# One pass over eight experts in the loop body, with the experts' rows spread by two fp32r products and weighted by VectorE

## Chip, cores, metric

The kernel runs on one core of a Trainium2 chip. The time is device microseconds of one execution; the kernel before took 3247.16 us in the median of three runs (3246.65 to 3254.41). The core has TensorE (PE), VectorE (DVE), ScalarE (ACT), GpSimd (POOL) and SyncE (SP), which here issues the weight transfers.

## The reference

The program is four transformer layers over 256 tokens of width 1024. Only the last part of the last layer matters here, a mixture of eight experts with the best two per token:

```
logits = h2 @ w_router                       # 256 x 8
top_logits, top_idx = top_k(logits, 2); top_w = softmax(top_logits)
for the tokens xs of each expert e:
    hid = silu(xs @ w_gate[e]) * (xs @ w_up[e])      # 1024 -> 3584
    y   = hid @ w_down[e]                            # 3584 -> 1024
    out[token] += y * top_w[token, e]
h = layer_norm(alpha * h + out)
```

Everything is fp32 in and out.

## The kernel before

**Weights.** All weights stream through the core in tiles of four 128-row blocks by 512 columns (1 MiB). SyncE issues one transfer a tile into a ring of four raw buffers (RAW, L611), once VectorE has used the tile that lay there (low_ready). fp32 products are made of fp32r parts: ScalarE rounds the tile to its high part (high_part, L1194), VectorE subtracts to get the low part (low_part, L1594), each into a ring of three (SPLIT). The activations are split the same way. TensorE then makes three products per 128x128 block: high by high (L641), low by high (L642), high by low (L643), that is 12 products of 128x512 a tile (tile_products).

**Route.** The route stage computes the logits, for each token the two experts, their weights (ROUTE[.., 2, ..]) and the token's slot in its expert's list (ROUTE[.., 3, ..]), and NPASS: 1 if no expert has more than 128 tokens, else 2. A pass takes at most 128 tokens of each expert.

**Experts.** One expert is 42 tiles: seven blocks of 512 hidden columns, each with two tiles of gate, two of up and two of down. The down tiles of a block come behind the gate and up tiles of the next one. All engines run the same loop (Fori) over pairs of experts: passes * 4 iterations with two experts written out in the body, PAIR = 84 tiles. m counts experts and is a register value plus a constant; so are the values of most waits. The ring positions don't depend on the iteration. SyncE computes the expert's index at run time.

For each expert, VectorE makes the choice matrix (choose, L2409): CHOICE[token, slot] is 1 where the token is in that slot. A second pair of operations multiplies it by the token's weight (CHOICEW, L2413). Behind the hidden product of block 1 it does this for the next expert. At the four last tiles of an expert TensorE gathers the next expert's rows, X times CHOICE, in two groups of 16 recorded products (L1106), and turns CHOICEW (L1114) into CHOICET, which ScalarE copies (L1541). ScalarE and VectorE split the gathered rows into XG high and low.

At the end of an expert ScalarE copies the down result from banks 6 and 7 to YE (L1571) and raises down_read. In the next expert's tiles 3 to 6, one step ahead of each, TensorE makes spread s: one fp32 product 128x512, CHOICET times half of YE, into bank 5 (L1121; it is recorded as two matmuls). VectorE adds the bank to MERGED (L2425), the accumulator of the layer. The last expert's four spreads follow the loop, into banks 0 to 3. In the first expert the spreads work on zeros, which route wrote by memset into YE and CHOICET (L2353, L2354).

**Order.** Each engine runs its own instruction stream in order, and semaphores join them. On ScalarE the copy to YE stands ahead of the high part of the next tile, number 44 counted from the expert's first; on VectorE the low part runs two tiles ahead of TensorE.

Of the kernel before, what the change touches and what calls it, by code (L numbers as in the profile page):

```python
# [26 lines left out]
P = 128  # L27
# [7 lines left out]
RAW = 4  # L35
# [236 lines left out]
def build(nc, a, out, const_at):  # L272

    stages = schedule()
    with ExitStack() as ctx:
# [163 lines left out]
        hid_turned = sem("hidden_turned")  # L439
        down_read = sem("down_read")  # L440
# [119 lines left out]
        PAIR = 2 * (3 * J * 2)  # L560
        SPREAD_AT = 3
        GATHER_AT = PAIR // 2 - 4
        assert PAIR % RAW == 0 and PAIR % SPLIT == 0

# [25 lines left out]
        def _(sp):  # L590
# [12 lines left out]
            for st in stages:  # L603
                if st["kind"] == "experts":
                    def load(h, expert, done=0):

                        tile = st["tiles"][h % (PAIR // 2)]
# [20 lines left out]
        def _(pe):  # L628
# [465 lines left out]
            def experts(st):  # L1094
# [15 lines left out]
                def turn_choice(m, bank=5):  # L1110
                    if bank == 5:
                        pe.wait_ge(gathered_read, m * 2 + 2)
                    for t in range(T):
                        tr = nc.tensor.transpose(PS[:, bank, t * P:(t + 1) * P], CHOICEW[:, t, :], ident)  # L1114
                    tr.then_inc(choice_turned, 1)

                def spread(m, half, s, bank=5):
# [3 lines left out]
                    nc.tensor.matmul(PS[:, bank, :], CHOICET[:, half, s // 2, :], YE[:, s % 2, :], start=True,  # L1121
# [7 lines left out]
                with pe.Fori(0, passes * (N_EXPERTS // 2)) as i:  # L1129
                    for half in range(2):  # L1130
                        m = i * 2 + half
                        for n, tile in enumerate(st["tiles"]):
                            h = STATIC + half * (PAIR // 2) + n
                            j = tile["block"]
                            par = (half * J + j) % 2
# [5 lines left out]
                            if SPREAD_AT <= n < SPREAD_AT + 4:  # L1141
                                spread(m, 1 - half, n - SPREAD_AT)
# [7 lines left out]
                            if turned_block:  # L1150
                                tb = turned_block["block"]
                                pe.wait_ge(xh_ready, m * J + tb + 3)
                                for x in range(4):
                                    tr = nc.tensor.transpose(PS[:, 4, x * P:(x + 1) * P],
                                                             HID2[:, (half * J + tb) % 2, x * P:(x + 1) * P], ident)
                                tr.then_inc(xh_turned, 1)
                            if tile["role"] != "down":
                                if tile["k"] == 0:
# [5 lines left out]
                                              tile["k"] == 0, tile["last"], i * PAIR)  # L1164
                            else:
                                if tile["first"]:
                                    pe.wait_ge(xh_copied, m * J + j + 1)
                                tile_products(h, tile, [PS[:, 6 + tile["half"], :]],
                                              lambda part, k, t: HIDT2[part][:, par, k, :], j == 0, j == J - 1, i * PAIR)
# [15 lines left out]
        def _(act):  # L1185
# [345 lines left out]
            def experts(st):  # L1531
                act.drain().then_inc(down_read, 1)

# [15 lines left out]
                with act.Fori(0, passes * (N_EXPERTS // 2)) as i:  # L1549
                    for half in range(2):  # L1550
                        m = i * 2 + half
                        for n, tile in enumerate(st["tiles"]):
                            h, j = half * (PAIR // 2) + n, tile["block"]
                            par = (half * J + j) % 2
                            if n in (GATHER_AT, GATHER_AT + 1):
                                gather(m + 1, n - GATHER_AT)
                            if n == GATHER_AT + 2:
                                copy_choice(m + 1, 1 - half)
                            turned_block = block_to_turn(st["tiles"], n)
                            if turned_block:  # L1560
                                tb = turned_block["block"]
                                act.wait_ge(xh_turned, m * J + tb + 1)
                                nc.scalar.activation(HIDT2[0][:, (half * J + tb) % 2].rearrange("p k s -> p (k s)"),
                                                     PS[:, 4, :], ACT.Copy).then_inc(xh_high, 1)
                            ahead = h + SPLIT - 1
                            high_part(STATIC + ahead, st["tiles"][ahead % (PAIR // 2)], (i * (PAIR // RAW), i * PAIR))
                            if tile["role"] == "gate" and tile["last"]:
                                act.wait_ge(tile_used, i * PAIR + STATIC + h + 1)
                                nc.scalar.activation(SG2[:, par], PS[:, par], ACT.Silu).then_inc(xsilu_ready, 1)
                        act.wait_ge(tile_used, i * PAIR + STATIC + (half + 1) * (PAIR // 2))  # L1570
                        nc.scalar.activation(YE.rearrange("p b c -> p (b c)"), PS[:, 6:8].rearrange("p b c -> p (b c)"),  # L1571
# [933 lines left out]
```

## Time and profile before

| | |
|---|---|
| median of three runs | 3247.16 us (3246.65 to 3254.41) |
| the profiled execution | 3250.54 us, its span 3248.7 us, mean granted clock 0.985 |
| TensorE busy | 3092.7 us, 95% |
| weight loads busy | 2526.1 us, 78% |
| VectorE busy | 2298.4 us, 71% |
| ScalarE busy | 1757.2 us, 54% |
| DMA | 697.25 MB, mean 215 GB/s |
| chain that ended last | PE 75%, DVE 10%, DMA 5%, ACT 4%, DVEq 3%, issue 3% |
| moe weight transfers | 114 gate, 112 up, 112 down, 1024 KB each |

The page's shares are means over the whole program. The experts stage begins near 2184 us and ends near 3232 us, so that it is a third of the span, and rows of that stage have to be asked for by their time. Matmul durations overlap: a 128x512 product is recorded with 390 ns, but one starts every 227 ns.

### The profile page before, as it was taken

To read this page: it belongs to the slowest core of one execution; us is meant where nothing else is said; L and a number is where in the kernel's file an instruction comes from. 1 tells how busy PE (TensorE), PEld (TensorE's weight loads), DVE (VectorE), ACT (ScalarE), POOL (GpSimd) and SP (SyncE) were. 2 spreads that over 40 slices of the span, in tenths; PEclk is the share of its full clock that TensorE was granted. 3 is DMA by queue.
4 is the path that set the end of the run, shared out by engine and by line. 5 is a ranking of instruction groups with operands and counts; after the bars stand their busy time and mean duration, and the time that the engine had idled before them with its cause. 6 is when DMAs were issued, how large, how long until landed. Compare 5 with 4: busy or idle time off the path is not lost.

```text
span 3248.7 us, 38581 instructions
## 1 busy us (share of the span) xinstructions
PE 3092.7 (95%) x15010; PEld 2526.1 (78%) x15010; DVE 2298.4 (71%) x2134; ACT 1757.2 (54%) x1647; POOL 46.1 (1%) x28
## 2 busy tenths in 40 slices
PE   8999999999998999999989999979999999999998
PEld 6777887877887787777878877767787787877876
DVE  7886556886556556765455667658887887887888
ACT  4564445465444444553334445536676676766765
POOL 0000000100000000000000000000000000000000
PEclk9999999999999999999999999989999999999999
DMA  6434555434555454335554543339998998999997
GB/s 242 143 130 145 187 183 175 159 117 135 183 185 188 157 169 156 130 112 180 189 168 157 181 154 123 113 118 339 334 362 304 350 354 302 358 338 312 364 327 266
DMA packets 351081, 697.25 MB, mean 215 GB/s; under 512 B 12225, under 2 KB 17217, under 8 KB 350785
## 3 DMA queue, kind: packets, MB, share of 16 engines
q1 hardware_dynamic: 347024, 687.75, 61.8%
q10 hardware_dynamic: 3888, 7.07, 0.7%
q8 instruction: 128, 2.10, 0.3%
q14 instruction: 41, 0.33, 0.0%
HBM read 693.73 MB, written 1.05 MB: 214 GB/s over the span
## 4 chain that ended last, share of the span: by engine, by line
PE 75%; DVE 10%; DMA 5%; ACT 4%; DVEq 3%; issue 3%; PEld 0%; ACTq 0%; POOL 0%; PEldq 0%; SPq 0%
PE banks L641 22%; PE banks L643 21%; PE banks L642 21%; DVE weights_low L1594 4%; ACT weights_high L1194 2%; DMA weights_raw<-in_moe_w_down_dram 2%; PE banks L796 1%; DMA weights_raw<-in_moe_w_up_dram 1%; DMA weights_raw<-in_moe_w_gate_dram 1%; PE banks L678 1%; PE banks L1106 1%; PE banks L1121 1%; PE banks L753 1%; ACT weights_transposed L1373 1%; PE banks L782 1%
## 5 line engine op out<-in xcount | busy, mean ns | idle before, releaser
L1594 DVE TENSOR_TENSOR weights_low<-weights_raw,weights_high 128x2048 fp32r<-128x2048 f32 (+1 forms) x658 | 1490.7, 2269 | 532.5 <-ACT weights_high L1194 526.8
L1194 ACT ACTIVATE weights_high<-weights_raw 128x2048 fp32r<-128x2048 f32 (+1 forms) x658 | 1247.7, 1898 | 578.4 <-PE banks L643 454.2
L641 PE MATMUL banks<-weights_high,h_transposed_high 128*128 128x512 f32 x2784 | 1122.6, 403 | 28.7 <-DVE weights_low L1594 15.3
L643 PE MATMUL banks<-weights_high,h_transposed_low 128*128 128x512 f32 x2784 | 1087.9, 391 | 11.5 <-issue 11.5
L642 PE MATMUL banks<-weights_low,h_transposed_high 128*128 128x512 f32 x2784 | 1086.0, 390 | 0.0
L641 PEld LDWEIGHTS banks<-weights_high,h_transposed_high 128*128 128x128 f32 x2784 | 527.5, 189 | 163.4 <-issue 23.5
L643 PEld LDWEIGHTS banks<-weights_high,h_transposed_low 128*128 128x128 f32 x2784 | 526.9, 189 | 123.8 <-issue 12.8
L642 PEld LDWEIGHTS banks<-weights_low,h_transposed_high 128*128 128x128 f32 x2784 | 527.9, 190 | 109.4 <-issue 8.6
L641 PE MATMUL banks<-weights_high,y_transposed_high 128*128 128x512 f32 x1096 | 433.5, 396 | 9.1 <-DVE y_transposed_low L2446 4.6
L643 PE MATMUL banks<-weights_high,y_transposed_low 128*128 128x512 f32 x1096 | 427.2, 390 | 0.0
L642 PE MATMUL banks<-weights_low,y_transposed_high 128*128 128x512 f32 x1096 | 427.0, 390 | 0.0
L641 PEld LDWEIGHTS banks<-weights_high,y_transposed_high 128*128 128x128 f32 x1096 | 205.8, 188 | 60.9 <-DVE weights_low L1594 7.3
L643 PEld LDWEIGHTS banks<-weights_high,y_transposed_low 128*128 128x128 f32 x1096 | 205.7, 188 | 43.7
L642 PEld LDWEIGHTS banks<-weights_low,y_transposed_high 128*128 128x128 f32 x1096 | 206.0, 188 | 40.6
L1368 ACT ACTIVATE scratch<-scratch,minus_row_max 128x256 f32<-128x256 f32 (+1 forms) x128 | 56.7, 444 | 67.4 <-DVEq L2033 67.4
L2478 POOL TENSOR_TENSOR rsqrt<-mean_squares,minus_half 128x2 f32<-128x2 f32 (+3 forms) x23 | 45.8, 1991 | 3195.7 <-DVE mean_squares L2259 1617.6
L1334 ACT ACTIVATE qk_transposed<-banks 128x512 f32<-128x512 f32 x68 | 38.8, 570 | 64.3 <-PE banks L737 60.0
L1307 ACT ACTIVATE projected<-banks 128x512 f32<-128x512 f32 x34 | 20.3, 596 | 97.3 <-PE banks L643 97.3
L1250 ACT ACTIVATE h_transposed_high<-banks 128x512 fp32r<-128x512 f32 x32 | 17.9, 596 | 95.6 <-PE banks L678 95.6
L1498 ACT ACTIVATE y_transposed_high<-banks 128x1024 fp32r<-128x1024 f32 (+1 forms) x22 | 22.2, 1007 | 87.4 <-PE banks L1044 87.4
L2319 DVE TENSOR_TENSOR y_transposed_low<-banks,y_transposed_high 128x1024 fp32r<-128x1024 f32 (+1 forms) x22 | 26.4, 1200 | 58.9 <-ACT y_transposed_high L1498 58.9
L796 PE MATMUL banks<-projected,weights_transposed 128*128 128x64 f32 (+1 forms) x384 | 49.7, 279 | 15.6 <-ACT weights_transposed L1373 15.6
(308 smaller groups left out, 2068.2 us busy)
## 6 DMA issues: line engine op xcount, KB each, us to landing
weights_raw<-in_w_in_dram SPq DMA_DIRECT2D x152, 1024.0 KB, 5.0
weights_raw<-in_moe_w_gate_dram SPq DMA_DIRECT2D x114, 1024.0 KB, 6.6
weights_raw<-in_moe_w_up_dram SPq DMA_DIRECT2D x112, 1024.0 KB, 6.5
weights_raw<-in_moe_w_down_dram SPq DMA_DIRECT2D x112, 1024.0 KB, 6.4
weights_raw<-in_w_up_dram SPq DMA_DIRECT2D x32, 1024.0 KB, 5.6
weights_raw<-in_w_down_dram SPq DMA_DIRECT2D x32, 1024.0 KB, 5.0
weights_raw<-in_ffn_w_gate_dram SPq DMA_DIRECT2D x10, 1024.0 KB, 5.1
weights_raw<-in_ffn_w_up_dram SPq DMA_DIRECT2D x10, 1024.0 KB, 5.1
```

The costliest lines, as they stand in the source:

```text
L641: nc.tensor.matmul(out_of[t], lhs(0, k, t), high[:, k], start=begin, stop=False)
L642: nc.tensor.matmul(out_of[t], lhs(0, k, t), low[:, k], start=False, stop=False)
L643: mm = nc.tensor.matmul(out_of[t], lhs(1, k, t), high[:, k], start=False, stop=end)
L678: tr = nc.tensor.transpose(PS[:, t["banks"][b], at:at + P], buf[t["src"]][:, i, t["cols"][k]:t["cols"][k] + P], ident)
L753: mm = nc.tensor.matmul(PS[:, 5 + h, cols], z[rows, q * P:(q + 1) * P], zk[rows, S:S + keys], start=True, stop=True)
L782: tr = nc.tensor.transpose(PS[:, 5 + h, i * P:(i + 1) * P], SM[:, h, i * P:(i + 1) * P], ident)
L796: mm = nc.tensor.matmul(PS[:, 7, o:o + vw], PT[:, h, (kt + t) * P:(kt + t + 1) * P], PR[:, kt, v0[h]:v0[h] + vw], start=kt == 0, stop=kt == t)
L1194: nc.scalar.activation(tile_view(WH, h % SPLIT, tile), tile_view(raw, h % RAW, tile), ACT.Copy).then_inc(high_ready, 1)
L1334: nc.scalar.activation(QKT[:, (n - 1) % 2, 0:cols], PS[:, bank, 0:cols], ACT.Copy).then_inc(qk_copied, 1)
L1368: nc.scalar.activation(probs, probs, ACT.Exp, bias=NMX[:, i:i + 1], accum_out=SUM[:, i:i + 1])
L1594: v.tensor_tensor(tile_view(WL, h % SPLIT, tile), tile_view(raw, h % RAW, tile), tile_view(WH, h % SPLIT, tile).bitcast(F32), ALU.subtract ...
L2478: nc.gpsimd.tensor_tensor(RSTD[:, 0:n], STAT[:, 0:n], MHALF[:, 0:n], ALU.pow).then_inc(rsqrt_ready, 1)
```

## The change

The loop body becomes all eight experts (PASS = 336 tiles, EXPERT = 42), and the loop runs once per pass, which here is once. The expert's index is then a constant for each transfer. The spread uses CHOICE without the weight, turned, in fp32r, and YE in a high part (ScalarE) and a low part (VectorE): two fp32r products in place of one fp32 product. VectorE multiplies by the weight while it accumulates. YE now lies in the upper halves of the HT buffers and CHOICET in a part of YT. The memsets in route go; zeroing by a multiplication with 0 stands at the head of the experts stage instead. down_read is raised by VectorE, behind its subtraction, which waits for the new semaphore down_high.

```diff
-        YE = PRf[:, 4096:5120].rearrange("p (b c) -> p b c", b=2)
+        YE = [h.rearrange("p k s -> p (k s)")[:, 1024:2048].rearrange("p (b c) -> p b c", b=2) for h in HT]
-        CHOICEW = PRf[:, 5376:5632].rearrange("p (t s) -> p t s", t=T)
-        CHOICET = PRf[:, 5632:6144].rearrange("p (b t s) -> p b t s", b=2, t=T)
+        CHOICET = YT[0].rearrange("p k s -> p (k s)")[:, 1024:1536].rearrange("p (b t s) -> p b t s", b=2, t=T)
...
-        PAIR = 2 * (3 * J * 2)
+        EXPERT = 3 * J * 2
+        PASS = N_EXPERTS * EXPERT
...
-                    with sp.Fori(0, passes * (N_EXPERTS // 2)) as i:
-                        for h in range(SPLIT - 1, PAIR + SPLIT - 1):
-                            load(h, (i * 2 + h // (PAIR // 2)) % N_EXPERTS, i * PAIR)
+                    with sp.Fori(0, passes) as i:
+                        for h in range(SPLIT - 1, PASS + SPLIT - 1):
+                            load(h, h // EXPERT % N_EXPERTS, i * PASS)
...
-                        tr = nc.tensor.transpose(PS[:, bank, t * P:(t + 1) * P], CHOICEW[:, t, :], ident)
+                        tr = nc.tensor.transpose(PS[:, bank, t * P:(t + 1) * P], CHOICE[:, t, :], ident)
...
-                    nc.tensor.matmul(PS[:, bank, :], CHOICET[:, half, s // 2, :], YE[:, s % 2, :], start=True,
+                    nc.tensor.matmul(PS[:, bank, :], CHOICET[:, half, s // 2, :], YE[0][:, s % 2, :], start=True, stop=False)
+                    nc.tensor.matmul(PS[:, bank, :], CHOICET[:, half, s // 2, :], YE[1][:, s % 2, :], start=False,
                                      stop=True).then_inc(spread_full, 1)
...
-                with pe.Fori(0, passes * (N_EXPERTS // 2)) as i:
-                    for half in range(2):
-                        m = i * 2 + half
+                with pe.Fori(0, passes) as i:
+                    for e in range(N_EXPERTS):
+                        m = i * N_EXPERTS + e
...
-                        nc.scalar.activation(YE.rearrange("p b c -> p (b c)"), PS[:, 6:8].rearrange("p b c -> p (b c)"),
-                                             ACT.Copy).then_inc(down_read, 1)
+                        nc.scalar.activation(YE[0].rearrange("p b c -> p (b c)"), PS[:, 6:8].rearrange("p b c -> p (b c)"),
+                                             ACT.Copy).then_inc(down_high, 1)
...
-                v.memset(YE, 0.0)
-                v.memset(CHOICET[:, 1], 0.0)
...
+                for part in YE:
+                    v.tensor_scalar(part.rearrange("p b c -> p (b c)"), MERGED[:, 0], 0.0, None, ALU.mult)
+                v.tensor_scalar(CHOICET[:, 1].rearrange("p t s -> p (t s)"), MERGED[:, 0, 0:T * P], 0.0, None, ALU.mult)
+                dve.drain().then_inc(down_read, 1)
...
-                    dve.drain()
-                    for t in range(T):
-                        v.tensor_scalar(CHOICEW[:, t], CHOICE[:, t], ROUTE[:, t, 2, bass.ds(at, 1)], None, ALU.mult)
                     dve.drain().then_inc(choice_ready, 1)
...
-                    v.tensor_tensor(acc, acc, PS[:, bank], ALU.add).then_inc(spread_read, 1)
+                    last = (m + T * N_EXPERTS - 1) % (T * N_EXPERTS)
+                    v.scalar_tensor_tensor(out=acc, in0=PS[:, bank], scalar=ROUTE[:, s // 2, 2, bass.ds(last, 1)], in1=acc,
+                                           op0=ALU.mult, op1=ALU.add).then_inc(spread_read, 1)
...
+                        dve.wait_ge(down_high, m + 1)
+                        v.tensor_tensor(YE[1].rearrange("p b c -> p (b c)"), PS[:, 6:8].rearrange("p b c -> p (b c)"),
+                                        YE[0].rearrange("p b c -> p (b c)").bitcast(F32), ALU.subtract).then_inc(down_read, 1)
```

## Rows read from the trace of the kernel before

**Rows 1.** page, 40 slices of the span: busy tenths of DMA
```profile
DMA  6434555434555454335554543339998998999997
```

**Rows 2.** windows from spread to spread: busy us by engine, clock, DMA share
```profile
2193.80:2323.30 129.50, 126.74 (x575) 102.17 (x574) 108.83 (x67) 89.80 (x61) 0.00 (x0) 1.00 0.96 341
2323.30:2457.60 134.30, 128.44 (x575) 103.34 (x574) 108.56 (x67) 92.22 (x62) 0.00 (x0) 0.99 0.94 334
...
2847.50:2983.90 136.40, 130.00 (x576) 102.82 (x575) 108.63 (x66) 92.24 (x62) 0.00 (x0) 0.99 0.94 328
2983.90:3111.00 127.10, 125.79 (x575) 102.40 (x574) 108.61 (x67) 89.73 (x61) 0.00 (x0) 1.00 0.97 342
```

**Rows 3.** waits, experts stage: total us, times, longest
```profile
DVE weights_low L1594 <- ACT weights_high L1194: 169.0, 242, 4.8
...
PEld banks L641 <- DVE weights_low L1594: 29.0, 42, 1.9
```

**Rows 4.** chain of waits, 2240 to 2266 us: start, us, what
```profile
2252.62 7.64 DMA weights_raw<-in_moe_w_down_dram
...
2260.28 1.93 ACT weights_high L1194
...
2262.23 2.30 DVE weights_low L1594
```

**Rows 5.** chain of waits at the three returns of the loop
```profile
2445.03 3.85 issue
...
2450.57 0.43 PE banks L641
...
2706.18 1.09 issue
...
2708.68 3.58 issue
...
2971.17 4.06 issue
```

**Rows 6.** windows of 20 us around a return, and without one
```profile
2439.00:2459.00 20.00, 15.75 (x60) 11.86 (x59) 11.18 (x6) 13.86 (x10) 0.00 (x0) 0.91 0.69 237
...
2309.00:2329.00 20.00, 20.00 (x87) 15.63 (x86) 17.24 (x10) 15.17 (x11) 0.00 (x0) 1.00 0.92 328
```

**Rows 7.** timeline at the choice, VectorE then TensorE
```profile
2214.16 0.60 DVE L2409 TENSOR_SCALAR projected<-constants,projected 128x128 f32<-128x128 f32 x2
2214.94 0.49 DVE L2413 TENSOR_SCALAR projected<-projected 128x128 f32<-128x128 f32 x2 [0.19 <-issue]
2215.62 4.49 DVE L1594 TENSOR_TENSOR weights_low<-weights_raw,weights_high 128x2048 fp32r<-128x2048 f32 x2 [0.19 <-issue]
...
2217.97 0.50 PE L641 MATMUL banks<-weights_high,h_transposed_high 128*128 128x512 f32 x1 [0.88 <-DVE weights_low L1594]
```

**Rows 8.** chain of waits at a spread
```profile
2323.47 0.86 PE banks L1121 x2
...
2324.80 0.23 PE banks L643
```

**Rows 9.** groups by line of VectorE: count, busy us, mean ns
```profile
L2319 DVE TENSOR_TENSOR y_transposed_low<-banks,y_transposed_high 128x1024 fp32r<-128x1024 f32 x21 | 25.7, 1225 | 57.5 <-ACT y_transposed_high L1498 57.5
...
L2425 DVE TENSOR_TENSOR merged<-merged,banks 128x512 f32<-128x512 f32 x36 | 24.6, 684 | 3.2 <-PE banks L1121 3.2
...
L2268 DVE SCALAR_TENSOR_TENSOR x_residual<-x_residual,rsqrt,scratch 128x512 f32<-128x512 f32 x16 | 11.3, 749 | 0.7
```

**Rows 10.** chain of waits in the route stage
```profile
2169.12 0.91 DVE projected L2353
```

**Rows 11.** timeline of VectorE after the loop
```profile
3234.72 0.69 DVE L2425 TENSOR_TENSOR merged<-merged,banks 128x512 f32<-128x512 f32 x1 [0.17 <-PE banks L1121]
```

**Rows 12.** DMA queues: packets, MB, share; 2190 to 2405 us, then 2405 to 3218
```profile
q14 instruction: 6, 0.05, 0.1%
...
q8 instruction: 37, 0.61, 0.3%
```

More of the change, by code:

```diff
@@ L559, in build @@
         STATIC = h
-        PAIR = 2 * (3 * J * 2)
+        EXPERT = 3 * J * 2
+        PASS = N_EXPERTS * EXPERT
         SPREAD_AT = 3
-        GATHER_AT = PAIR // 2 - 4
-        assert PAIR % RAW == 0 and PAIR % SPLIT == 0
+        GATHER_AT = EXPERT - 4
+        assert PASS % RAW == 0 and PASS % SPLIT == 0
         def tile_view(buffer, slot, tile):
@@ L605, in load @@
                     def load(h, expert, done=0):
-                        tile = st["tiles"][h % (PAIR // 2)]
+                        tile = st["tiles"][h % EXPERT]
                         src = a[tile["name"]][tile["layer"], bass.ds(expert, 1), tile["row"]:tile["row"] + tile["rows"] * P,
@@ L1141, in experts @@
                             if SPREAD_AT <= n < SPREAD_AT + 4:
-                                spread(m, 1 - half, n - SPREAD_AT)
+                                spread(m, 1 - e % 2, n - SPREAD_AT)
                             if n == GATHER_AT:
@@ L1163, in experts @@
                                 tile_products(h, tile, [PS[:, bank, :]], lambda part, k, t: XG[part][:, tile["k"] + k, :],
-                                              tile["k"] == 0, tile["last"], i * PAIR)
+                                              tile["k"] == 0, tile["last"], i * PASS)
                             else:
@@ L1548, in experts @@
                 passes = act.value_load(NPASS[0:1, 0:1], min_val=1, max_val=T)
-                with act.Fori(0, passes * (N_EXPERTS // 2)) as i:
-                    for half in range(2):
-                        m = i * 2 + half
+                with act.Fori(0, passes) as i:
+                    for e in range(N_EXPERTS):
+                        m = i * N_EXPERTS + e
                         for n, tile in enumerate(st["tiles"]):
-                            h, j = half * (PAIR // 2) + n, tile["block"]
-                            par = (half * J + j) % 2
+                            h, j = e * EXPERT + n, tile["block"]
+                            par = (e * J + j) % 2
                             if n in (GATHER_AT, GATHER_AT + 1):
@@ L1557, in experts @@
                             if n == GATHER_AT + 2:
-                                copy_choice(m + 1, 1 - half)
+                                copy_choice(m + 1, 1 - e % 2)
                             turned_block = block_to_turn(st["tiles"], n)
@@ L2430, in experts @@
                 passes = dve.value_load(NPASS[0:1, 0:1], min_val=1, max_val=T)
-                with dve.Fori(0, passes * (N_EXPERTS // 2)) as i:
-                    for half in range(2):
-                        m = i * 2 + half
+                with dve.Fori(0, passes) as i:
+                    for e in range(N_EXPERTS):
+                        m = i * N_EXPERTS + e
                         for n, tile in enumerate(st["tiles"]):
-                            h, j = half * (PAIR // 2) + n, tile["block"]
-                            par = (half * J + j) % 2
+                            h, j = e * EXPERT + n, tile["block"]
+                            par = (e * J + j) % 2
                             if SPREAD_AT <= n < SPREAD_AT + 4:
```

24 lines of the change are left out of this document (12 added, 12 removed).

## The prediction

> **What bounds the kernel now.** I read the page's row of DMA shares first, then the stage in eight equal steps, then who waits for whom, then the chain of waits inside one step, and last the edges of the loop. The reader is to see this. Up to about 2184 us the sixteen DMA engines are half busy; in the last third, the experts stage, they are at eight or nine tenths nearly all the time [rows 1]. That stage is the only thing that the change touches. From the first spread of one expert to that of the next there are seven stretches, of which the first two and the last two stand in [rows 2]. Four of the seven (129.5, 129.7, 126.5, 127.1 us, mean 128.2) hold no return of the loop. Three (134.3, 133.7, 136.4, mean 134.8) do. TensorE is busy nearly throughout, and DMA at 0.94 to 0.97.
>
> So two things bound one expert in turn. TensorE needs 504 products of 0.227 us (a 128x512 product takes 0.23 of the chain [rows 8]), which is 114.4 us, plus gather 3.6 (two groups of 1.78 us), turning the hidden block 7 x 0.36 = 2.5, turning the choice 0.14 and the spread 3.4: together some 124 us. DMA needs 42 tiles of 1 MiB. At 0.965 busy over 128.2 us [rows 2] that is 123.7 us of full work. The two floors are almost equal, and an expert takes 128.2 because each is late for the other in turn. In the DMA's part the ring of four raw tiles is what one sees: a transfer of 7.6 to 7.9 us, then ScalarE's rounding 1.93, VectorE's remainder 2.30, and the next transfer starts [rows 4]. That is 12.3 us for four tiles, 3.08 each, where TensorE would take 2.72. Around the gathers and spreads TensorE is the slower one and the DMA share falls to about 0.9 [rows 6]. VectorE waits for ScalarE's high parts for 169 us in all, and TensorE waits for VectorE's low parts for 29 us, 3.6 an expert [rows 3].
>
> **The loop's returns.** The body of the loop covers two experts, runs four times, and so returns three times. At each, TensorE stands with the reason "issue": nothing that another engine did ended it. It is 3.85, 3.58 and 4.06 us [rows 5], with a shorter piece before it (0.39, 1.09, 0.5). Behind it the clock is granted at half for 3.4 us (products at 0.43 instead of 0.23 us in the chain [rows 5]), which loses 1.7 us more. Sum: 4.24 + 4.67 + 4.56 + 3 x 1.7 = 18.6 us. The stretches say the same from outside: 3 x (134.8 - 128.2) = 19.8. The body becomes eight experts and NPASS is 1 here (336 tiles were run), so no return is left. But while TensorE stood, the DMA idled only in part: share 0.69, 0.66, 0.71 in 20 us around the returns against 0.92, 0.86, 0.92 at the same place of an expert without one [rows 6], 0.213 x 20 = 4.3 us each, 12.8 in all. The rest of the pause was used to fill the ring. The gain therefore lies between 12.8 and 19.8. I take 17, nearer the upper end, because TensorE is what works directly behind the return, with spreads to do.
>
> Two ScalarE table loads of 1.28 us per body go from eight to two; they lie beside TensorE's pause and I cost them at nothing of their own. They would matter only if ScalarE were late, and it waits for TensorE or DMA.
>
> **The spread.** One fp32 product 128x512 is recorded as two, 0.86 us in the chain [rows 8]. It becomes two fp32r products. The trace has no spread of that kind; its nearest rows are the weight products, which are fp32r of the same shape: 0.227 each, 0.453 for both. Bounds: 0.45 if it is like those, 0.86 if nothing is gained. I take 0.453, saving 0.41 x 4 = 1.65 us an expert, 13.1 us in the eight that run inside the loop.
>
> **VectorE.** Accumulating becomes a scalar_tensor_tensor with a column of weights. Its neighbours are tensor_tensor at 0.68 and, with a column, 0.75 us [rows 9]: 0 to 0.07 more, 36 times, 2.4 us at most, beside TensorE's next tile. The register work for the column runs in the queue ahead of the engine. New is the low part of the down result: 128x1024 from PSUM, 1.22 us [rows 9], once an expert. It waits for ScalarE's copy. Behind it on VectorE stands the low part of tile 44, and for that TensorE waits. If TensorE ends tile 41 at T, ScalarE's copy ends at T+1.03, the subtraction at T+2.3 (VectorE may still be in tile 43's low part until about T+1.7, then T+2.9), while the high part of tile 44, behind the same copy on ScalarE, ends at T+2.95. So the subtraction fills time in which VectorE waits anyway, and TensorE has tiles 42 and 43 in hand, 5.4 us. Cost 0. If that cover is gone it is 2.25 us an expert, 18 in all.
>
> Off VectorE goes the weighted choice: two 128x128 operations and a drain. The chosen pair starts at 2214.16, the weighted pair at 2214.94, the next low part at 2215.62 [rows 7], so 0.68 us go. This is on the path: TensorE stands for about 1.04 us behind that low part (0.88 shown by the row, since its last product's modelled end overlaps [rows 7]), and does so once in every expert. I expect 0.36 of it to stay: 8 x 0.68 = 5.4 us gained. Bounds 0 and 8.3.
>
> **Edges.** In the route stage a memset of 0.91 us [rows 10] and a smaller one behind it leave VectorE's path, about 1.1 us. Two zeroings of 128x1024 and one of 128x256 come before the first choice, where the first gather waits for them: 1.7 by estimate: the trace has no scaling of that size into such an operand; the subtraction of 128x1024 at 1.22 us [rows 9] is the upper bound of each large one, its half the lower, and I take near the lower with a drain. The first choice is 0.7 shorter. Sum 0, between -0.5 and +1.3. At the end, the last spread now waits for the subtraction too (+1.2), and VectorE's four accumulations, 0.86 apart today since it waits for each product [rows 11], come 0.65 apart: -0.8. Sum +0.5.
>
> **The sum.** TensorE's side: 17 + 13.1 + 5.4 - 0.5 = 35. What of the 18.5 us of spread and choice remains after the DMA? An expert without a return would need 128.2 - 2.3 = 125.9 us, and DMA cannot do it in less than 123.7. So it fits, but the part of an expert in which the ring fills gets 2.3 us shorter, and the DMA idles only 4.5 us an expert today. In that part the DMA is at 0.9, so of a microsecond saved there most is not yet a DMA microsecond; later, in the ring's own part, some is waited for again. I take 60 per cent, between 0 and 100: 11 us. Total 17 + 11 - 0.5 = 27.5, rounded 28. The profiled execution took 3250.5 us (span 3248.7), so 3222.5. It lies 3.4 us above the median of the runs shown (3247.2); the forecast for that median is **3219**. Its own range is 3211 to 3228.
>
> **Rivals.**
> (a) *The DMA takes back all but its own idling.* For it: share 0.965 already, the 12.3 us ring. Against: it does fall to 0.9 at the spreads. Gain 12.8, time 3234. Chance 0.20.
> (b) *All of TensorE's side counts.* For it: the ring is full after every slow part. Against: 29 us of waits for low parts are left over today. 19.8 + 18.5 - 0.5 = 37.8, time 3209. Chance 0.20.
> (c) *VectorE's new wait isn't covered.* Low part of tile 44 comes 2.25 us late each time and the weight column costs 0.07 x 36: 28 - 18 - 2.4 leaves 8, time 3239. For it: VectorE is at 0.84 of a stretch. Against: ScalarE's order above. Chance 0.06.
> (d) *The longer program makes the engines wait for their code; slower than before.* The queue that brings 8 KB packets of code (q14) moved 0.05 MB, six packets, in the first 215 us of the loop, and has no row at all from 2405 to 3218, whereas TensorE's (q8) goes on with 37 of 16 KB [rows 12]. ScalarE, VectorE and SyncE thus ran bodies two to four from code they held. Now they need 3 x 6 = 18 more packets. If each came as late as TensorE's page at a return (3.85 us [rows 5]) that is 69 us; with half of it covered by the two tiles in hand, 35, and 3219 + 35 = 3254. It decides from 28 / 18 = 1.6 us a packet. Against: the first two experts did fetch theirs, in 129.5 us for the first, the same as the 129.7 of the third, which did not. Chance 0.04.
>
> Rows 12 and the pauses of rows 5 belong together: code is brought in pages, and TensorE's alone is too long to be kept. [...]
>
> **Chances.** Forecast 0.50, (a) 0.20, (b) 0.20, (c) 0.06, (d) 0.04. Changes within 0.3 per cent, about 9.7 us, can't be told from none by a measurement of this kernel: 3237.4 is the border. Faster: 0.50 + 0.20 + most of (a), 0.17 = 0.87. Same: rest of (a) 0.03, (c) 0.05 = 0.08. Slower: (d) and what is left = 0.05. The range reaches from below (b) to just past (a): 3205 to 3237.
>
> **What would show it.** In the changed profile: no "issue" of 3 to 4 us on TensorE and no half clock between 2190 and 3220; spread products of the weight products' duration, two a spread, and a tile with a spread in it 0.41 us shorter; a stall of about 0.4 instead of 1.04 after the choice; a new 128x1024 subtraction eight times with nothing of TensorE or of the low parts waiting for it; DMA share at 0.97 or more in each stretch; experts of 125 to 127.5 us. Experts of 128 with more waits for DMA show (a). "Issue" on VectorE, ScalarE or the DMA queue's engine at regular places, with packets on q14, shows (d). The prediction is wrong if experts take under 124 us, which would mean that the DMA can do more than I take for full, or over 129.

## The result and the profile after

The changed kernel takes 3211.26 us (median of four runs, 3206.66 to 3215.40) against 3247.25 us beside it. The ratio is 0.9877 with a 95 per cent interval of 0.9857 to 0.9897, so it is faster by 1.2 per cent. The medians lie 36 us apart, the ratio makes it 40 us (33 to 46), and 28 were forecast. The two profiled executions have spans of 3248.7 and 3209.3 us, 39.4 us apart. The terms below are compared on these two.

The page of the changed kernel: span, busy time, the DMA's busy tenths in 40 slices (now nine from the twenty-ninth on, where [rows 1] had eights), and the queue that brings code to the engines other than TensorE.

```profile
span 3209.3 us, 37966 instructions
...
PE 3073.3 (96%) x15010; PEld 2523.9 (79%) x15010; DVE 2302.4 (72%) x2125; ACT 1750.2 (55%) x1641; POOL 46.1 (1%) x28
...
DMA  6434555443565554335555543338999999999997
...
q14 instruction: 55, 0.45, 0.0%
```

The seven stretches of the experts stage, cut from ScalarE's copy of one down result to that of the next (columns: length, PE, PEld, DVE and ACT busy, POOL, granted clock, DMA share, GB/s):

```profile
2312.40:2437.30 124.90, 124.65 (x575) 102.12 (x575) 109.38 (x66) 89.61 (x61) 0.00 (x0) 1.00 0.99 353
2437.30:2562.60 125.30, 124.63 (x576) 102.30 (x575) 109.20 (x66) 89.60 (x61) 0.00 (x0) 1.00 0.99 352
2562.60:2687.70 125.10, 124.72 (x576) 102.10 (x575) 109.17 (x66) 89.89 (x61) 0.00 (x0) 1.00 0.99 353
2687.70:2813.60 125.90, 124.98 (x575) 101.98 (x574) 109.22 (x66) 89.98 (x61) 0.00 (x0) 1.00 0.99 350
2813.60:2940.30 126.70, 124.76 (x575) 102.07 (x574) 109.34 (x66) 89.65 (x60) 0.00 (x0) 1.00 0.99 348
2940.30:3065.50 125.20, 124.67 (x576) 102.25 (x575) 109.23 (x66) 89.49 (x61) 0.00 (x0) 1.00 0.99 353
3065.50:3191.00 125.50, 124.69 (x574) 101.82 (x572) 109.13 (x66) 89.61 (x60) 0.00 (x0) 1.00 0.95 338
```

Three of the same cuts in the kernel before: one without a return of the loop, one with, and the last.

```profile
2315.20:2443.20 128.00, 126.39 (x575) 101.96 (x573) 108.60 (x67) 89.45 (x60) 0.00 (x0) 1.00 0.97 345
2443.20:2579.20 136.00, 128.92 (x576) 103.50 (x576) 108.80 (x67) 92.30 (x62) 0.00 (x0) 0.99 0.93 325
3103.00:3231.60 128.60, 126.63 (x574) 101.67 (x572) 108.83 (x67) 89.46 (x60) 0.00 (x0) 1.00 0.92 329
```

Before, the seven were 128.0, 136.0, 127.0, 133.3, 129.9, 133.6 and 128.6 us, 916.4 in all. Now they are 124.9 to 126.7, 878.6 in all. So 37.8 of the 39.4 us are here. The stretches are the better measure than the spans: what lies ahead of the experts stage, where the kernels differ only in how they clear YE and CHOICET, moves its start by up to 5.6 us from one profile to another (first gather at 2175.8 to 2181.4 us). Each kernel has one profile, and single stretches without a return differ by up to 3.5 us inside one profile (123.5 to 127.0 in one_product below), so that a sum of seven is good to a few us only. The clock column reads 1.00 in every stretch. The DMA share is 0.99, against 0.93 to 0.97 before, and in the last stretch, where the loads end, 0.95 against 0.92. This answers to [rows 2, 6].

Who waits for whom in the stage (total us, times, longest), against [rows 3]. The pauses of 3.6 to 4.1 us by "issue" of [rows 5] are gone; what is left of that kind sums to 2.9 us and is never longer than 0.5.

```profile
DVE weights_low L1594 <- ACT weights_high L1196: 127.2, 220, 3.1
...
PEld banks L642 <- DVE weights_low L1594: 20.8, 41, 1.6
...
PEld banks L642 <- issue: 2.9, 7, 0.5
```

The chain of waits at a spread. Two products of 0.23 us stand where [rows 8] had 0.86:

```profile
2323.60 0.23 PE banks L644
2323.82 0.23 PE banks L1122
2324.05 0.23 PE banks L1123
2324.28 0.23 PE banks L642
```

VectorE's timeline at the choice, and TensorE's behind it, against [rows 7]. From the choice to the next low part it is 0.80 us instead of 1.46, and TensorE's stall has shrunk to 0.21 us by the row (0.37 from start to start, where it was 1.04):

```profile
2338.55 0.68 DVE L2454 TENSOR_TENSOR projected<-projected,banks 128x512 f32<-128x512 f32 x1
2339.14 0.60 DVE L2411 TENSOR_SCALAR projected<-constants,projected 128x128 f32<-128x128 f32 x2
2339.94 4.50 DVE L1594 TENSOR_TENSOR weights_low<-weights_raw,weights_high 128x2048 fp32r<-128x2048 f32 x2 [0.20 <-issue]
```

```profile
2342.29 0.50 PE L642 MATMUL banks<-weights_high,h_transposed_high 128*128 128x512 f32 x1 [0.21 <-DVE weights_low L1594]
```

### The profile page after: what moved, and what is told of

Read it like the earlier page. It is cut to its first block, busy times and chain, and to the rows that moved or that the text cites. A ratio compares the mean times of both kernels' runs of the same rounds, so it can differ in the third digit from the quotient of the medians.

```text
span 3209.3 us, 37966 instructions
## 1 busy us (share of the span) xinstructions
PE 3073.3 (96%) x15010; PEld 2523.9 (79%) x15010; DVE 2302.4 (72%) x2125; ACT 1750.2 (55%) x1641; POOL 46.1 (1%) x28
## 4 chain that ended last, share of the span: by engine, by line
PE 76%; DVE 10%; DMA 4%; ACT 4%; DVEq 3%; issue 2%; PEld 0%; ACTq 0%; POOL 0%; PEldq 0%
PE banks L642 22%; PE banks L644 22%; PE banks L643 22%; DVE weights_low L1594 4%; ACT weights_high L1196 2%; DMA weights_raw<-in_moe_w_up_dram 2%; PE banks L797 1%; DMA weights_raw<-in_moe_w_down_dram 1%; PE banks L679 1%; PE banks L1107 1%; DMA weights_raw<-in_moe_w_gate_dram 1%; PE banks L754 1%; ACT weights_transposed L1375 1%; PE banks L783 1%; PE banks L1045 1%
## 5 line engine op out<-in xcount | busy, mean ns | idle before, releaser
L642 PE MATMUL banks<-weights_high,h_transposed_high 128*128 128x512 f32 x2784 | 1107.9, 398 | 21.2 <-DVE weights_low L1594 9.7
```

The source lines that it names most:

```text
L642: nc.tensor.matmul(out_of[t], lhs(0, k, t), high[:, k], start=begin, stop=False)
```

## The experts' parts: the returns and the spread

**The body alone (loop_only).** The loop runs once over eight experts. Everything about spread and choice is the old code.

```diff
-                with pe.Fori(0, passes * (N_EXPERTS // 2)) as i:
-                    for half in range(2):
+                with pe.Fori(0, passes) as i:
+                    for e in range(N_EXPERTS):
```

> Body of eight experts, the spread as before (fp32 product of the weighted choice, memsets in route). Theory A, TensorE's time counts whole: the three returns are worth the difference of the stretches, 19.8 us, so some 3227 us (18.6 to 20 off the kernel before). Theory B, the DMA idles only in part at a return and the rest is taken back: 12.8 us, 3234. Theory C, most of the 36 us measured for the whole change come from the returns and the spread is nearly free of effect: 28 us or more, under 3220.

Measured: ratio 0.9916 (0.9901 to 0.9931), median 3228.12 us. The profiled span is 3227.1 us. The seven stretches are 129.3, 128.5, 127.2, 127.4, 128.5, 127.9 and 126.7 us, 895.5 in all, 20.9 less than before; no half clock lies between them. Theory A holds by the stretches (19.8 expected). By the ratio it is 27 us, 22 to 32, which is more than A says; these runs stood beside runs of the kernel before that spread from 3246 to 3261 us. Theory B's 12.8 us lies outside the interval and is far from the stretches; C falls with the next kernel.

**The spread alone (spread_only).** The changed kernel with a body of two experts.

```diff
-        PASS = N_EXPERTS * EXPERT
+        BODY = 2
+        PASS = BODY * EXPERT
...
-                with pe.Fori(0, passes) as i:
-                    for e in range(N_EXPERTS):
-                        m = i * N_EXPERTS + e
+                with pe.Fori(0, passes * (N_EXPERTS // BODY)) as i:
+                    for e in range(BODY):
+                        m = i * BODY + e
```

> The new spread, weight column and shorter choice, but the body of two experts with its three returns. Theory A: 1.65 + 0.68 us an expert, 18 us off the kernel before, 3229 us. Theory B, the DMA takes most of it back: 0 to 8 us, 3240 to 3247. Theory C: under 8 us. If the two parts hold each other up (each alone is worth less than its share because the other bound stands), this and the body of eight alone sum to less than the whole change's 36 us; if they take from the same slack, to more.

Measured: median 3234.22 us (3228.20 to 3243.62), ratio 0.9945 (0.9926 to 0.9964), 18 us, 12 to 24; span 3230.3 us, 18.4 less. That is theory A's number, and B and C are out. The stretches say more. Without a return they are 126.4, 124.6, 126.0 and 125.1 us, mean 125.6, which is 2.8 less than the 128.4 before. With one they are 133.8, 133.9 and 134.2, mean 134.0, against 134.3 before. So a return costs 8.4 us here and cost 5.9 there. The spread's gain is whole wherever there is no return and does not show where there is one: 12.2 us in the seven, and the two parts alone sum to 33.1 where the whole change has 37.8. By the ratios (27 and 18 against 40) the difference would not be seen.

Two things are longer at the returns of this kernel. The half clock behind each lasts 6.8 us (3.4 before), which costs 1.7 us more. And the pauses are 4.40, 4.35 and 4.03 us against 3.85, 3.58 and 4.06 in [rows 5]. The first in the chain of waits (start, us, what):

```profile
2434.53 0.63 issue
...
2436.57 4.40 issue
```

That the new spread makes the half clock longer is not shown: it is also 6.8 us at all three returns of ring_before and at two of the three of choice_only, and both have the old spread.

**One return instead of three (body_four).** BODY = 4 in the same edit.

> The changed kernel with a body of four experts, so one return of the loop in place of none. Theory A: one return costs 6.3 to 6.6 us, 3217.7 us against 3211.3, with one pause by issue of about 4 us on TensorE and one stretch of half clock. Theory B: 4.3 us, 3215.5. No return cost at all, or three times as much, would mean that the pauses aren't what the body's length removes.

Measured: 3219.46 us, ratio 0.9895 (0.9879 to 0.9912), which overlaps the changed kernel's. The trace is clearer: 126.7, 123.9, 125.4, **134.1**, 125.4, 124.0 and 124.3 us. Only the stretch with the return is long, by 9.1 us over the mean of the others, with one pause of 3.96 us and one stretch of half clock (6.8 us). The seven sum to 883.8 against 878.6. So it is 5.2 us net, between B's 4.3 and A's 6.3 (6 us by the ratios), while the stretch by itself costs more than either. The other six average 125.0, the changed kernel's seven 125.5. A ring filled in the pause would explain that for the three behind it, but the three ahead of it are as short, so it is not shown.

**The choice alone (choice_only).** The kernel before, with the weight applied while accumulating and CHOICE turned without it; the spread stays one fp32 product.

```diff
-                    dve.drain()
-                    for t in range(T):
-                        v.tensor_scalar(CHOICEW[:, t], CHOICE[:, t], ROUTE[:, t, 2, bass.ds(at, 1)], None, ALU.mult)
                     dve.drain().then_inc(choice_ready, 1)
...
-                    v.tensor_tensor(acc, acc, PS[:, bank], ALU.add).then_inc(spread_read, 1)
+                    v.scalar_tensor_tensor(out=acc, in0=PS[:, bank], scalar=ROUTE[:, s // 2, 2, bass.ds(last, 1)], in1=acc,
+                                           op0=ALU.mult, op1=ALU.add).then_inc(spread_read, 1)
```

> The kernel before with one part of the change: the weight is applied by VectorE while it accumulates and the weighted choice is gone; the spread stays one fp32 product, no low part, body of two experts. Theory A, the stall behind the choice is on the path: 0.68 us an expert, 5.4 us, 3242 us, TensorE's stall at the choice 0.36 in place of 1.04 us. Theory B, the time is taken back by the DMA a few tiles later: 0 to 1 us. Theory C, it is worth more than 5.4 because VectorE's lead carries over: 8 us.

Measured: ratio 0.9982 (0.9970 to 0.9994), 2 to 10 us; span 3243.4, 5.3 less. Every choice stall went from 1.04 to 0.37 us, and the stretches sum to 912.2, 4.2 less where seven times 0.68 would be 4.8. Theory A. The interval excludes B's 0 to 1 us; alone it would not exclude C.

## What the DMA costs, before and after

The forecast lost 7.5 us to the DMA by an argument. The kernels of this section look for that loss.

**A TensorE edit in the changed kernel (one_product).** The second product of each spread is gone, and with it the low part of the down result from the sum.

```diff
-                    nc.tensor.matmul(PS[:, bank, :], CHOICET[:, half, s // 2, :], YE[0][:, s % 2, :], start=True, stop=False)
-                    nc.tensor.matmul(PS[:, bank, :], CHOICET[:, half, s // 2, :], YE[1][:, s % 2, :], start=False,
+                    nc.tensor.matmul(PS[:, bank, :], CHOICET[:, half, s // 2, :], YE[0][:, s % 2, :], start=True,
                                      stop=True).then_inc(spread_full, 1)
```

> The changed kernel without the second product of each spread (the low part of the down result is left out of the sum; the subtraction that makes it stays). 32 products of 0.227 us inside the loop are gone. Theory A, TensorE's time still counts whole in the changed kernel: 7.3 us faster, 3204 us. Theory B, the changed kernel is at the DMA's bound (share 0.98 or so): 0 to 2 us faster.

Measured: median 3205.79 us, ratio 0.9858 (0.9838 to 0.9878), overlapping the changed kernel's 0.9857 to 0.9897. The spans differ by 2.4 us, and the seven stretches not at all: 878.5 against 878.6, although 6.4 us of products are gone from them. That is theory B's number, but two things weaken it. The ratios alone (6 us apart, with overlapping intervals) would not exclude A's 7.3. And a new wait takes part of the saving before the DMA can: with one product a spread, TensorE's fourth spread waits for VectorE's accumulation in every stretch, 0.37 us from start to start.

```profile
PEld banks L1122 <- DVE merged L2424: 4.4, 7, 0.6
```

So only about half of the 6.4 us was there to be gained (3.0 in ring_one_product below, which has the same wait). That this half did not show fits the DMA's side, in one profile each.

**Half the bytes (half_loads, half_loads_before).** In the experts stage each transfer brings two of four row blocks. The other half of a raw buffer keeps old weights; all computing stays.

```diff
-                        src = a[tile["name"]][tile["layer"], bass.ds(expert, 1), tile["row"]:tile["row"] + tile["rows"] * P,
+                        src = a[tile["name"]][tile["layer"], bass.ds(expert, 1), tile["row"]:tile["row"] + 2 * P,
```

> The changed kernel with transfers of half a tile in the experts stage (two of four row blocks; the other half of each raw buffer keeps old weights, all computing stays). It takes the DMA out of the bound. Theory A: TensorE's own sum, 122.7 - 1.65 = 121.0 us and the 0.36 us left of the choice stall: stretches of 121 to 122 us, 25 to 36 us faster than the changed kernel. Theory B, the 4 us an expert above TensorE's sum come from ScalarE and VectorE splitting just in time and not from the DMA: stretches of 124 to 125.5, 0 to 10 us faster.

> The kernel before with the same halved transfers. With no DMA bound, the whole change must be worth TensorE's side: three returns at 18.6 us, spreads 13.1, choice 5.4. Theory A: the distance to the changed kernel with half loads is 36 to 38 us, as with full loads (39.4 us between the two profiled spans), stretches of 123.5 us and 129.8 to 130.5 with a return. Theory B, the DMA took back a part with full loads: the distance is 45 us or more.

Measured: half_loads 3198.51 us, ratio 0.9831 (0.9812 to 0.9850), span 3198.5, stretches of 123.9 to 124.0, 867.7 in all. half_loads_before 3234.28 us, ratio 0.9946 (0.9927 to 0.9965), span 3229.3, stretches 126.4 without a return and 133.1, 131.2, 131.9 with one, 901.8 in all. The first kernel's stretches are theory B's number (124 to 125.5) and not A's 121 to 122, though it is 13 us faster by the medians where B says 0 to 10. B's reason, splitting just in time, isn't shown by it. The windows (columns as above) of one stretch of the first, and of two of the second, with a DMA share of 0.6:

```profile
2312.80:2436.80 124.00, 123.79 (x576) 102.43 (x576) 109.07 (x66) 89.54 (x61) 0.00 (x0) 1.00 0.60 178
```

```profile
2310.40:2436.80 126.40, 125.49 (x575) 102.16 (x573) 108.47 (x67) 89.43 (x60) 0.00 (x0) 1.00 0.59 175
2436.80:2569.90 133.10, 128.83 (x575) 104.85 (x576) 108.47 (x67) 92.23 (x63) 0.00 (x0) 0.97 0.56 166
```

TensorE's own expert is therefore 124.0 us now and was 126.4, not 121 and 124 as I had summed. Between both kernels it is 2.4 us: the 1.65 and 0.68 of the forecast. The distance of the two is 35.8 us between the medians (37 by the ratios), which is A's 36 to 38; in the stretches it is 34.1, and between these two spans 30.8, because what lies ahead of the first gather took 4.4 us longer in half_loads. B's 45 is far from all of them. The returns cost 5.7 us each here. The pauses are shorter than with all the bytes (3.58 to 4.06): in the chain of waits 3.02, 1.92 and 2.73 us. That a page of code comes sooner when the DMA is less busy is my reading of it:

```profile
2438.58 3.02 issue
...
2698.73 1.92 issue
...
2955.97 2.73 issue
```

**Six tiles in flight (ring_six, ring_before).** Two unused scratch buffers join the ring of raw tiles in this stage.

```diff
-                        sp.wait_ge(low_ready, STATIC + h - RAW + 1 + done)
-                        sp.dma_start(tile_view(raw, (STATIC + h) % RAW, tile), src).then_inc(landed[(STATIC + h) % RAW], 16)
+                        sp.wait_ge(low_ready, STATIC + h - (RAW if h < RAW else RING) + 1 + done)
+                        sp.dma_start(ring_view(h, tile), src).then_inc(landed[ring_slot(h)[0]], 16)
...
+            return (S0f, S1f)[r - RAW][:, 0:tile["rows"] * tile["width"]].rearrange("p (k c) -> p k c", k=tile["rows"])
```

> The changed kernel with six raw tiles in flight in the experts stage in place of four (the fifth and sixth lie in two scratch buffers that the stage doesn't use). Taking a product of each spread away from the changed kernel left its seven expert-to-expert stretches at 878.5 us against 878.6, so something other than TensorE sets them at 125.5 us each. Theory A, the ring of four does (transfer of 6 to 8 us, then 1.93 + 2.30 us of splitting before the next one starts): the DMA gets to 0.99 or more, stretches of 121.5 to 123.7 us, 14 to 32 us faster than the changed kernel, some 3185 to 3197 us. Theory B, the DMA's bandwidth does, with about 351 GB/s all it can give beside the rest: more in flight only makes each transfer last longer, stretches stay within 1 us, 3207 to 3212 us. Theory C, two more transfers in flight collide: slower.

Measured: 3198.05 us, ratio 0.9830 (0.9813 to 0.9846), whose interval lies wholly under the changed kernel's. It is the fastest complete kernel of this study. Seven stretches of 123.9 to 124.0 us, 867.7 in all, to the tenth those of half the bytes, at twice the bytes:

```profile
2310.30:2434.30 124.00, 123.79 (x575) 102.44 (x575) 109.07 (x66) 89.53 (x61) 0.00 (x0) 1.00 1.00 356
2434.30:2558.20 123.90, 123.70 (x575) 102.38 (x574) 108.95 (x66) 89.48 (x60) 0.00 (x0) 1.00 0.99 356
```

ScalarE now waits for TensorE and hardly for a transfer, and TensorE's weight loads wait 5.8 us for low parts in 2320 to 3180 us, where the changed kernel has 17.1 in the same window:

```profile
ACT weights_high L1216 <- PE banks L660: 124.3, 168, 1.3
...
PEld banks L658 <- DVE weights_low L1614: 5.8, 13, 0.6
```

So the ring of four bounded the changed kernel, by 1.6 us an expert on the mean, and not the DMA's bandwidth, which gave 356 GB/s here. Single stretches reach the same 124.0 us with four tiles (two in body_four, at 356 GB/s), so the ring of four is not late in every expert:

```profile
2441.20:2565.10 123.90, 123.70 (x575) 102.39 (x574) 109.02 (x66) 89.44 (x60) 0.00 (x0) 1.00 1.00 356
```

Theory A in its mechanism (the ratio is 15 us under the changed kernel's); its stretches were set too low, because TensorE's 124.0 stood nearer than the 121.5 to 123.7 that I had written.

> Six raw tiles in the kernel before: body of two experts, fp32 spread, weighted choice. Theory A, with six in flight only TensorE's side is left, as with half the bytes: stretches of 126.4 us and 131 to 133 with a return, seven together 902 us, 15 us faster than before, about 3234 to 3238 us. Theory B, the returns get dearer because a full DMA delays the pages of code more: stretches with a return of 134 or more, 5 to 9 us faster than before.

Measured: 3238.96 us, ratio 0.9952 (0.9937 to 0.9968), span 3237.2. Stretches of 126.4 without a return, as A says, and 134.0, 133.6 and 135.0 with one, near B's 134: 7.8 us a return where half the bytes gave 5.7. The 8.3 us of the stretches (916.4 to 908.1) are B's number, while the ratio gives 16 us (10 to 21), which is A's 15 and excludes B's 5 to 9. The two are not reconciled. Nor is B's reason shown. Of the 7.8 us, 3.4 are lost to a half clock of 6.8 us at each return, where the kernel before lost 1.7; that is nearly all of the difference to its 5.9. The pauses are 3.83, 4.62 and 4.07 us, 0.3 more on the mean.

**Both (ring_one_product).** ring_six without the second product.

> Six raw tiles, and the second product of each spread left out (the low part of the down result isn't added). With six tiles the stretches were 124.0 us, to a tenth the same as with half the bytes, so TensorE alone sets them; the DMA ran at 0.98 and 351 GB/s. Theory A, TensorE still sets them: 4 x 0.227 = 0.9 us less a stretch, 123.1 us, 861.3 us for the seven in place of 867.7. Theory B, at 124 us the DMA's bandwidth stands right behind: 123.5 to 124.0 us.

Measured: 3192.53 us, ratio 0.9811 (0.9793 to 0.9828), not distinct from ring_six. Stretches of 123.5 to 123.6, 864.7 in all: 3.0 of the 6.3 us. That is B's number, but not cleanly its reason, for a third thing appears, VectorE. The stall of 0.37 us of one_product stands in the spreads of every stretch here too, and explains most of the 0.5 us an expert that is missing from A's 0.9. TensorE's fourth spread waits for VectorE's accumulation:

```profile
PEld banks L1138 <- DVE merged L2444: 4.6, 8, 0.7
```

Whether the DMA's bandwidth would come next stays open; at 123.5 us an expert it gave 357 to 358 GB/s at a share of 0.99 to 1.00.

## The edit that I costed at nothing

**subtract_twice.** VectorE's new subtraction runs twice, the first time into a scratch buffer.

```diff
+                        v.tensor_tensor(S1f[:, 0:1024], PS[:, 6:8].rearrange("p b c -> p (b c)"),
+                                        YE[0].rearrange("p b c -> p (b c)").bitcast(F32), ALU.subtract)
                         v.tensor_tensor(YE[1].rearrange("p b c -> p (b c)"), PS[:, 6:8].rearrange("p b c -> p (b c)"),
```

> The changed kernel with VectorE's new subtraction doubled at its place (the first of the two writes to a scratch buffer), 1.22 us more once an expert, in front of the low part of tile 44. Theory A, it is covered by ScalarE's high part and by the two tiles that TensorE has in hand: stretches of 125.5 us and the median within 1 us of the changed kernel. Theory B, VectorE's time at this place is on the path: up to 1.2 us a stretch, 8 to 10 us slower.

Measured: 3217.65 us, ratio 0.9892 (0.9875 to 0.9910), overlapping the changed kernel's; span 3217.2, 7.9 more, stretches 884.9, 6.3 more. Theory B in its kind, with less than its 8 to 10 us in the stretches; the stall described below, which A denies, stands in all seven. In the changed kernel, VectorE's and ScalarE's timelines at the end of an expert are these:

```profile
2438.74 1.22 DVE L2458 TENSOR_TENSOR h_transposed_low<-banks,h_transposed_high 128x1024 fp32r<-128x1024 f32 x1
2440.16 4.50 DVE L1594 TENSOR_TENSOR weights_low<-weights_raw,weights_high 128x2048 fp32r<-128x2048 f32 x2 [0.20 <-ACT weights_high L1196]
```

```profile
2437.29 1.03 ACT L1571 ACTIVATE h_transposed_high<-banks 128x1024 fp32r<-128x1024 f32 x1 [0.80 <-PE banks L644]
2438.22 3.72 ACT L1196 ACTIVATE weights_high<-weights_raw 128x2048 fp32r<-128x2048 f32 x2
```

The subtraction ends and VectorE still waits 0.20 us for the high part of tile 44. That is the cover, and it is thin. Doubled, the low part starts at 2441.39 and not some 0.2 us after the high part; it ends at 2443.68, and TensorE, whose two tiles in hand are used up, stands. It does so in every stretch, 0.8 us from start to start:

```profile
2439.13 1.22 DVE L2458 TENSOR_TENSOR scratch<-banks,h_transposed_high 128x1024 f32<-128x1024 f32 x1
2440.26 1.22 DVE L2460 TENSOR_TENSOR h_transposed_low<-banks,h_transposed_high 128x1024 fp32r<-128x1024 f32 x1
2441.39 6.69 DVE L1594 TENSOR_TENSOR weights_low<-weights_raw,weights_high 128x2048 fp32r<-128x2048 f32 x3
```

```profile
2443.73 0.50 PE L642 MATMUL banks<-weights_high,h_transposed_high 128*128 128x512 f32 x1 [0.64 <-DVE weights_low L1594]
```

## Why the prediction was right, and where it was not

**Direction and mechanism** were right: returns, spread and choice all count on TensorE's path. 3211.3 us lies in the range, at the lower end of the likeliest case's own (3211 to 3228).

**The returns: 17 us forecast, 20.9 measured** in the stretches by loop_only, of which 17.6 are the returns themselves (mean 134.3 with one, 128.4 without) and 3.3 the other stretches. Whether the discount from 19.8 to 17 was wrong is not decided: the returns themselves measured 17.6, and the stretches without one differ by up to 2.6 us among themselves in loop_only. A return isn't a fixed price either: 5.7 us with half the bytes, 5.9 in the kernel before, 7.8 with six tiles, 8.4 and about 9 with the new spread. Much of that is the half clock behind it: 3.4 us long at all three returns of the kernel before, 6.8 at all of spread_only, body_four and ring_before, and both lengths stand in choice_only (6.8, 3.4, 6.8) and in half_loads_before (6.8, 3.4, 3.4). The longer one costs 1.7 us more. What decides between the two is open, but neither the new spread nor a full DMA is needed for it.

**Spread and choice: 18.5 us on TensorE forecast**, 2.3 an expert. Measured are 2.8 in the returnless stretches of spread_only and 2.9 in the changed kernel (128.4 to 125.5), some 20 in seven stretches, where the forecast's 2.3 make 16. With half the bytes it is 2.4 (126.4 to 124.0), the forecast's own term. The product's price (0.453 for 0.86), the 0.68 us and the 0.36 left over came out to a few hundredths.

**The step that failed is "I take 60 per cent".** Nothing was given back. I had put TensorE's own time at 124 us an expert and the DMA's at 123.7, so that over 4 us of each 128.2 had to be mutual waiting, for which a faster TensorE would pay. half_loads_before gives TensorE's time as 126.4. The sum had left out the choice stall of 1.04 us, although it stood a paragraph below, and about 1 us of later starts: eleven products a stretch start 0.31 to 0.34 us after the one before instead of 0.227. The DMA's 123.7 was nearly right, for the shortest stretches brought their 42 tiles in 123.5 us at a share of 1.00. The waiting for the DMA was 2.0 us an expert before (128.4 - 126.4) and is 1.6 now (125.5 - 124.0). The balance of the seven stretches, by the kernels with half the bytes: TensorE's own time 17.1 us less (7 x 126.4 = 884.8 to 867.7), the returns 17.0 less (901.8 - 884.8), the waiting for the DMA 3.7 less (14.6 to 10.9). Sum 37.8. Rival (b), all of TensorE's side, is what happened: 37.8 us forecast for the whole, 39.4 measured between the profiles, 36 between the medians and 40 by the ratio. That the seven stretches give 37.8 too is chance: (b)'s terms would be some 36 for them, and TensorE's side alone measured 34.1. My forecast stood because the range reached to it.

**Covered costs.** The subtraction costs nothing, as forecast, but only by the 0.2 us that it ends ahead of the high part (0.05 to 0.65 by the forecast's own times). The 5.4 us in hand that I named beside it gave no cover: 1.22 us more on VectorE stopped TensorE for 0.8 us in every stretch. Rival (c) was nearer than its chance of 0.06 suggests, though not at its price of 2.25 us. Accumulating takes 0.746 us against 0.682, as the bound said.

**Code.** Rival (d) was right in its premise and wrong in its price. The queue that had no packet behind 2405 us in [rows 12] now has 16 up to 3178, and 5 ahead of that (first line, 2190 to 2405 us; the other two, 2405 to 3178):

```profile
q14 instruction: 5, 0.04, 0.0%
...
q8 instruction: 29, 0.48, 0.2%
q14 instruction: 16, 0.13, 0.0%
```

I had expected 18 beyond the six of before. No engine shows a pause by "issue" of over 0.5 us for one, and TensorE's own queue (q8) brings its 29 packets without such a pause too. So the cost lay at the branch back, and not in a page as such. The Trainium skill, "Runtime: NRT & Kernel Launch", Instruction fetch mechanics, says that the fetch is sequential and mostly hidden, and that a taken branch whose target lies outside the two pages in hand has to wait for a fetch. The trace agrees here: pauses of 3.58 to 4.06 us at the three branches before, none in the seven stretches now. The short bodies of the other engines branched back before without a packet of code [rows 12].

**Edges.** From the first gather to the first copy it is 134.1 us, before 137.6: the 2.3 of the spread and choice and 1.2 more than I had. This part differs from profile to profile (134.7 us in loop_only, with nothing of spread or choice changed), so the 1.2 us may be no more than that. From the last copy of a down result to the end it is 18.2 us, before 17.1: 1.1 us more where I had 0.5. After the last subtraction VectorE accumulates four times in 3.00 us, waiting 1.00 us for the first product:

```profile
3192.49 1.22 DVE L2458 TENSOR_TENSOR h_transposed_low<-banks,h_transposed_high 128x1024 fp32r<-128x1024 f32 x1
3194.70 3.00 DVE L2425 SCALAR_TENSOR_TENSOR merged<-banks,projected,merged 128x512 f32<-128x512 f32 x4 [1.00 <-PE banks L1123]
```

## What to carry to other kernels

When two resources look equally full, don't argue how much one takes back from the other. Halve the bytes, or deepen the ring, and read the other's own time from the stretches. A loop's return on TensorE, with some 2400 instructions in the body, cost a stop of 3.6 to 4.6 us at full load and a half clock after it, and writing the loop out cost nothing here, since the longer code came in order. A wait that is "covered" needs its slack written down in tenths of a microsecond, from the work that stands behind it in the same queue.

## What the runs showed of the hardware

The pause at a return was shorter when the DMA was less busy: 1.92 to 3.02 us by the chain at a share of 0.6, 3.58 to 4.62 at full load. The packets of code stand on queues of the same sixteen DMA engines as the weights. The half clock behind a return lasted 3.4 or 6.8 us, in one and the same kernel too. The DMA engines held 356 GB/s in every stretch of 124 us at a share of 0.99 to 1.00 once six transfers of 1 MiB could be under way (the last apart, where the loads end), against 348 to 353 in the changed kernel with four. And a scalar_tensor_tensor from PSUM with a column of scalars takes 0.746 us for 128x512, against 0.682 for the plain sum.
